# A two-block transformer on one core: half of the second layer's memory values issued inside the attention of the first mixer, and that attention's outputs in one bank

## The reference, cut to what matters

```python
logits = einsum('bhqd,bhkd->bhqk', q_b, k) * scale + F_b[..., :, None] - F[..., None, :]   # 8 forgetting heads of 64
p = softmax(where(k_pos <= q_pos, logits, NEG_INF)); out = p @ v
p = softmax(l1 masked) - lam * softmax(l2 masked); d_out = p @ v                            # 4 differential heads of 128
d_out = rms_norm(d_out, subln) * (1.0 - lambda_init)
x = x + concatenate([fox_out, d_out]) @ w_out
k, v = split(rms_norm(mem, mem_norm[1]) @ wkv[1], 2)                                        # "memory values" is this v
```

## Time and profile before

| | us |
|---|---|
| median of 3 runs | 2553.18 |
| lowest and highest run | 2551.69, 2554.51 |
| span of the profiled execution | 2548.6 |
| TensorE busy | 2505.5 (98%) |
| VectorE busy | 1268.0 (50%) |
| ScalarE busy | 534.4 (21%) |
| GpSimd busy | 548.5 (22%) |

### The profile page before, as it was taken

One profiled execution on the slowest core, in us unless ns is written; L12 is line 12 of the kernel. 1 busy time (PEld: TensorE's weight loads), 2 busy tenths in 40 slices (PEclk: granted clock), 3 DMA queues, 4 the chain that ended last, 5 costly groups with the idle time before them and its releaser, 6 DMA issues.

```text
span 2548.6 us, 36840 instructions
## 1 busy us (share of the span) xinstructions
PE 2505.5 (98%) x14094; PEld 2037.0 (80%) x14094; DVE 1268.0 (50%) x2578; ACT 534.4 (21%) x1167; POOL 548.5 (22%) x474
## 2 busy tenths in 40 slices
PE   9989999999999999999999999999999999999999
PEld 6857899986799998645567766888888875899999
DVE  4034178751326887214746763545541237435774
ACT  1131122112212221112630001222200224212220
POOL 1000135100213530001002321323231001132543
PEclk9999999999999999999999999999999999999999
DMA  6323265644235565110014662122222130244442
GB/s 238 132 99 116 83 223 189 252 178 165 87 129 204 185 240 214 67 60 25 1 73 146 219 248 107 67 99 74 103 91 79 67 118 1 100 149 166 165 190 108
DMA packets 39971, 334.93 MB, mean 131 GB/s; under 512 B 3872, under 2 KB 10144, under 8 KB 22688
## 3 DMA queue, kind: packets, MB, share of 16 engines
q1 hardware_dynamic: 39840, 333.11, 35.4%
HBM read 332.04 MB, written 1.05 MB: 131 GB/s over the span
## 4 chain that ended last, share of the span: by engine, by line
PE 91%; DVE 3%; DMA 2%; POOL 1%; issue 1%; ACT 1%; SPq 0%; DVEq 0%; POOLq 0%
PE PS L767 25%; PE PS L567 20%; PE PS L1027 6%; PE PS L2700 6%; PE PS L1521 5%; PE PS L1711 4%; PE PS L2741 4%; PE PS L1336 3%; PE PS L1696 3%; PE PS L2272 2%; PE PS L1347 2%; PE PS L1359 2%; DMA slot<-in_weights 1%; PE PS L434 1%; PE PS L748 1%
## 5 line engine op out<-in xcount | busy, mean ns | idle before, releaser
L567 PE MATMUL PS<-XN,slot 128*128 128x256 f32 (+1 forms) x1184 | 296.8, 411 | 0.9 <-DMA slot<-in_weights 0.9
L767 PE MATMUL PS<-SQ,slot 128*128 128x128 f32 (+1 forms) x1984 | 294.2, 301 | 0.0
L567 PEld LDWEIGHTS PS<-XN,slot 128*128 128x128 f32 x1184 | 224.5, 190 | 69.9 <-issue 42.5
L767 PEld LDWEIGHTS PS<-SQ,slot 128*128 128x128 f32 x1984 | 268.1, 191 | 12.8
L767 PE MATMUL PS<-XN,slot 128*128 128x128 f32 (+1 forms) x1664 | 250.0, 301 | 0.0
L567 PE MATMUL PS<-arena,slot 128*128 128x256 f32 x1088 | 236.5, 379 | 1.0 <-DVE arena L1952 0.9
L767 PEld LDWEIGHTS PS<-XN,slot 128*128 128x128 f32 x1664 | 226.1, 192 | 10.7
L567 PEld LDWEIGHTS PS<-arena,slot 128*128 128x128 f32 x1088 | 206.4, 190 | 30.6 <-issue 2.0
L890 DVE SCALAR_TENSOR_TENSOR arena<-PS,small,arena 128x255 f32<-128x255 f32 (+2 forms) x352 | 174.9, 543 | 45.6 <-ACT arena L834 44.7
L834 ACT ACTIVATE arena<-PS,small 128x256 f32<-128x256 f32 (+1 forms) x176 | 105.4, 616 | 375.6 <-DVE PS L923 245.0
L478 POOL TENSOR_TENSOR SQ<-SQ 128x512 f32<-128x512 f32 (+1 forms) x36 | 42.6, 1189 | 538.7 <-ACT SQ L444 538.1
(11 more groups left out here) (286 smaller groups left out, 3692.0 us busy)
## 6 DMA issues: line engine op xcount, KB each, us to landing
slot<-in_weights SPq DMA_DIRECT2D x85, 2048.0 KB, 7.7
arena<-in_mod SPq DMA_DIRECT2D x96, 512.0 KB, 3.4
slot<-in_weights SPq DMA_DIRECT2D x16, 2816.0 KB, 9.6
slot<-in_weights SPq DMA_DIRECT2D x24, 1536.0 KB, 6.8
slot<-in_weights SPq DMA_DIRECT2D x5, 1024.0 KB, 4.9
slot<-in_weights SPq DMA_DIRECT2D x2, 2176.0 KB, 8.9
arena<-in_c SPq DMA_DIRECT2D x3, 1024.0 KB, 10.3
small<-in_small SPq DMA_DIRECT2D x1, 2301.0 KB, 18.0
```

The costliest lines, as they stand in the source:

```text
L567: mm = pe.matmul(o, l, r, start=k == 0, stop=k == len(terms) - 1, skip_group_check=True)
L767: mm = pe.matmul(PS[:, bank, 0:h], lhs[:, k * P:(k + 1) * P], rhs(k), start=first and k == 0, stop=last and k == 3, skip_group_check=True)
```

## The change

The 8 products of memv0 for the first half of the memory rows (`tensor_memv_first`) no longer stand behind the attention. `tensor_pairs` takes a function `fill` and calls it with u-2 ahead of each turn, so that one of the products stands ahead of each of the 8 turns, all into bank 7. The attention's outputs therefore all go to bank 6 (`out_bank`), for "fox" alone. ScalarE reads bank 7 directly behind the attention's last output (`scalar_memv`), and bank 3 behind subln. The 8 products for the second half (`tensor_memv_second`) stay between the subln sums and mixout0, in bank 3, with the last head's sum behind the fourth of them.

```diff
+        def out_bank(s, un):
+            return 6 if s == "fox" else 6 + un["out"] % 2
...
-                bank = 6 + un["out"] % 2
+                bank = out_bank(s, un)
                 if un["out_first"]:
                     claim(pe, bank)
...
                 if u >= 4:
                     values(u - 4)
                 if 2 <= u < len(units) + 2:
+                    if fill:
+                        fill(pe, u - 2)
                     turn(u - 2)
...
-                    act.activation(un["dst"], PS[:, 6 + un["out"] % 2, 0:T], ACT.Copy)\
+                    act.activation(un["dst"], PS[:, out_bank(s, un), 0:T], ACT.Copy)\
...
+                def tensor_memv_first(pe, k):
+                    if k == 0:
+                        claim(pe, 7)
+                    mm = pe.matmul(PS[:, 7, :], MEMN[1][:, k, 0:P], next_tiles(pe, 4), start=k == 0, stop=k == DK - 1,
+                                   skip_group_check=True)
+                    if k == DK - 1:
+                        mm.then_inc(*tick(TD, "memv0", "tok", 0))
+                        lend(7, ("memv0", "tokread", 0))
+                        Stream.tile = 0
+
+                def tensor_memv_second(pe, between):
+                    claim(pe, 3)
+                    for k in range(DK):
+                        mm = pe.matmul(PS[:, 3, :], MEMN[1][:, k, P:T], next_tiles(pe, 4), start=k == 0, stop=k == DK - 1)
+                        if k == DK // 2 - 1:
+                            between(pe)
+                    finish(mm, "memv0", "tok", 1)
+                    lend(3, ("memv0", "tokread", 1))
+
+                def scalar_memv(act, t, bank):
+                    act.wait_ge(*of("memv0", "tok", t))
+                    act.activation(VM[1][:, 4 * t:4 * t + 2, :], PS[:, bank, :].rearrange("p (b t) -> p b t", t=T), ACT.Copy)\
+                        .then_inc(*tick(SD, "memv0", "tokread", t))
...
                 add_pairs("fox", fox_units(), [("fox", "F"), ("lambda", "ready"), ("foxin", "read", 5, 0),
-                                               ("foxin", "read", 7, 0), ("foxin", "tokread", 3)])
+                                               ("foxin", "read", 7, 0), ("foxin", "tokread", 3)],
+                          fill=tensor_memv_first)
+                add(scalar=lambda a: scalar_memv(a, 0, 7))
...
-                    tensor_memory_values(pe, 0, between=lambda pe: tensor_norm(pe, "subln", un, 3))
+                    tensor_memv_second(pe, lambda pe: tensor_norm(pe, "subln", un, 3))
...
-                add(scalar=lambda a: scalar_memory_values(a, 0))
+                add(scalar=lambda a: scalar_memv(a, 1, 3))
```

More of the change, by code:

```diff
@@ L1325, in two_blocks, with tensor_pairs @@
         PT = [PTR, RT]
-        def tensor_pairs(pe, s, units, ready, early=None, late=None):
+        def out_bank(s, un):
+            return 6 if s == "fox" else 6 + un["out"] % 2
+        def tensor_pairs(pe, s, units, ready, early=None, late=None, fill=None):
             for label in ready:
@@ L1593, in add_attention, with add_pairs @@
                 gpsimd=lambda p: gpsimd_attention(p, s, units))
-        def add_pairs(s, units, ready=(), early=(None, ()), late=None):
-            add(tensor=lambda pe: tensor_pairs(pe, s, units, ready, early[0], late),
+        def add_pairs(s, units, ready=(), early=(None, ()), late=None, fill=None):
+            add(tensor=lambda pe: tensor_pairs(pe, s, units, ready, early[0], late, fill),
                 scalar=lambda a: scalar_pairs(a, s, units, early[1]),
```

## The result

| | before | changed |
|---|---|---|
| median, us | 2553.57 (4 runs) | 2574.18 (4 runs) |
| lowest and highest run | 2551.69, 2554.51 | 2570.38, 2574.73 |
| span of the profiled execution | 2548.6 | 2572.1 |
| ratio of the runs | | 1.0077, 95% interval 1.0063 to 1.0091 |

The change costs 20.6 us. The forecast was +12.8 and its range ended at 2571: the direction and the place were right, the size was not. The profiled execution of the changed kernel took 2573.85 us, 1.8 us more than its span.

What follows compares the result with a forecast made beforehand. TensorE's in-order queue was taken to bound the kernel. Subln beginning 15.8 us late, less 3.0 us given back, made +12.8 us, taking the median from 2553.18 to 2566.0 us; range 2561 to 2571.

Steps and rivals of the forecast that it cites:

- The moved products: Eight memory values products at 0.86 us each leave the block behind fox; 6.87 us leave it and enter fox.
- Two fills that no wait covers: Moved products ahead of turns 0 and 1 of fox, where PE had no idle time: 1.72 us of delay.
- One bank for all outputs: In fox, values of unit m wait for ScalarE's read of output m-1; largest term, turn 6 is 12.31 us late.
- the loop: In fox: turn, minima, exponentials, output, values, fill, next turn, through three engines; 6.31 us from turn to turn.
- ScalarE's read of bank 7: Between fox's last output and subln's first square: some 0.5 us more, so subln begins 15.8 us late.
- What the shorter block gives back: At mixout0: PE could come 6.87 us earlier, but needs the last result of VectorE's norm chain; gain 3.0 us.
- The expected wait of 3.6 us in mixout0: In mixout0's first group, PE stands some 3.6 us ahead of the product that needs subln's last result.
- The clock: PE's granted clock stays at 1.00 (2.4 GHz) throughout, also with the new loop's waits; no time was added.
- The second rival: In fox, behind waits longer than any in the trace, bursts run at 1.2 GHz: +5 to +13 us; chance 10%.
- its first case: Two bursts of fox's loop at 1.2 GHz: +5 us, giving 2571 us.
- The median, 4.6 us above the span: Whole kernel: the median of the runs, 2553.18 us, lies 4.6 us above the profiled span of 2548.6 us.

Runs made afterwards that it cites:

- e3: The changed kernel plus 52 products whose results nobody reads, in TensorE's waits ahead of fox's values products; 2568.08 us, ratio 1.0055.
- e2: The changed kernel with ScalarE's output read issued ahead of the turn copy and exponentials, for fox alone; 2555.35 us, ratio 1.0009.
- e0: The kernel before with ScalarE's output read issued earlier, two banks kept and no product moved; 2554.69 us, ratio 1.0000.
- e4: e2 with mixout0 issuing the products that need no subln result first, for all four tiles of its first slab; 2549.83 us, ratio 0.9985.
- e1: The kernel before with all fox outputs sent to bank 6 and no memory values product moved; 2566.87 us, ratio 1.0049.

## Why the prediction was wrong in size, point by point

- *The moved products, 6.87 us out of the block*: right. The block is 8 products; each costs 0.86 us at full clock.
- *Two fills that no wait covers, 1.72 us*: the second turn comes 1.68 us late, the third 1.58.
- *One bank for all outputs*: right in mechanism and size. With the clock kept (e3) the loop took 6.35, 6.24, 6.24, 6.69 us against 6.31 and 6.77; the last values products came 14.9 us late against the forecast's 15.3. Changing only the order of ScalarE's read (e2) took the loop away.
- *ScalarE's read of bank 7, 0.5 us*: 0.48.
- *What the shorter block gives back, 3.0 us and not 6.87*: right in sum. From the last values products to mixout0's end the change gains 2.4 us (22.5 to 20.1), which is 0.5 paid for the read and 3.0 gained, within 0.1. The expected wait of 3.6 us in mixout0 was 0.55, since PE had come late; in e2 and e3 it was 3.3. The low clock behind that wait, 1.7 us in e2, has no term in the forecast either.
- *The clock, "I take it as 1.00 throughout"*: **this is the step that failed.** It was priced at nothing and measures 22.5 - 14.9 = 7.6 us in fox. The forecast's +12.8 and this make 20.4, and 20.1 was found at mixout0's end, 20.6 in the medians. The second rival (the clock drops) is what happened; it had 10%, and its first case (two slow bursts, +5) was too mild, since all four loops from turn 2 to turn 6 had slow bursts.
- *The median, 4.6 us above the span for what lies around it*: a wrong reading, without effect on the forecast. Every run of which both are on record took 1.7 to 1.9 us more than its span, so the profiled execution of the kernel before took, by estimate, 2550.4 us (2548.6 + 1.8) and was a short one, 3.2 below the median of 2553.57.

The step failed on the choice of row. The earlier trace rows has PE at half load and the clock at 1.00, with waits of up to 1.6 us. But the same trace had a stretch with the clock down, and I had not looked for one, because the mean over the span was 0.999. It is the start of the first feed-forward layer, in the profile of the kernel before:

```profile
327.51 0.79 PE L748 MATMUL PS<-XN,slot 128*128 128x128 f32 x4 [0.84 <-DVE XN L506]
329.22 0.49 PE L748 MATMUL PS<-XN,slot 128*128 128x128 f32 x2 [0.92 <-DVE XN L506]
330.62 1.65 PE L748 MATMUL PS<-XN,slot 128*128 128x128 f32 x6 [0.92 <-DVE XN L506]
```

```profile
330.00:337.00 7.00, 6.38 (x31) 6.38 (x32) 6.62 (x12) 0.00 (x0) 0.28 (x1) 0.52 1.01 387
```

Behind three waits of 0.84 to 0.92 us, with bursts of 0.79 and 0.49 us between them, PE worked at 0.52 of its clock. So the second rival's condition, a wait longer than any in this trace, does not hold even there. Where the clock falls behind waits of 0.9 us, a loop with waits of 2.7 to 3.6 us could not be taken to keep it. The rule of the Trainium skill that I had set against the row (TensorE: Matmul & The Clock Gate, "HAM oscillation — how this bites in real kernels") says that a PE which waits too long between its bursts starts the next one throttled. The changed kernel agrees with it (0.50 to 0.52 behind waits of 2.74 and 3.59 us), and so does e3 (1.00 once the waits are filled).

A low clock costs only where PE is on the path. In fox PE's turn, values and fill are parts of the loop, and the minima wait for the turn: the 7.6 us were paid. In the memory values block of the changed kernel 2.6 us (6.18 - 3.60) were not, because subln's chain on VectorE was the longer one. In mixout0 of e2 and e3 it was paid again, 1.6 to 1.7 us (26.56 and 26.51 against 24.87).

The two profiled spans differ by 23.5 us, and the medians by 20.6. The 2.9 us between are the two executions that happened to be profiled: that of the kernel before was 3.2 us below its median, that of the changed kernel 0.3 below. They come in at several places behind 808 us. e0 is like it: equal to the kernel before until 360 us, its profiled execution is 3.0 us longer in span, at the same median. What makes single executions differ so is open; no run separates it.

## What to carry to other kernels

A buffer given up closes a loop through whoever frees it, at the place where that read stands in its own engine's queue: before taking a PSUM bank away, move the read that frees it ahead of the long work in front of it (here that alone was worth 18 us, e2 against the changed kernel). Where an estimate puts waits of some microseconds between TensorE's bursts, price the bursts behind them at half clock too, and look through the whole trace for the stretch with the lowest granted clock. A block of work that covers another engine's chain can only be shortened together with that chain, or with the order of those who wait for it. Here the move with the read ahead alone ended 2.3 us late at mixout0's end (e2), and with the new order 3.2 us early (e4).

## What the runs showed of the hardware

- With the same wait of 2.73 us, the first one in e1 was followed by a turn of 0.88 us and the second by one of 1.54: whether the clock falls is not decided by the one wait alone.
- Products that nobody reads, in TensorE's waits, held the granted clock at 1.00 where it had been 0.72 on the mean of 170 to 205 us, and made the kernel 5 to 6 us faster while adding 52 products. They write the last 128 columns of a scores bank, which nobody reads, and no semaphore orders them behind VectorE's read of the bank's other columns: in e3 that read ends at 173.24 us (172.82 + 0.42, L1438), and the first of them starts at 173.21. A kernel that is to be kept should order the two.
- A hand-over from ScalarE to TensorE took 0.06 us in the loop (in the changed kernel read over at 175.57 + 0.36, products from 175.99), against the 0.14 from VectorE on which the forecast counted.
